# A matmul-heavy two-block kernel on one core: the second product of both MLPs by Strassen's seven block products

## The reference

```python
u = rmsnorm(h, mlp_norm_g[layer])
h = h + jnp.square(jax.nn.relu(u @ w_ff1[layer])) @ w_ff2[layer]   # 1024 -> 4096 -> 1024
```

## Time and profile before

| | |
|---|---|
| median of 3 runs | 3369.88 us (3363.81 to 3376.24) |
| profiled execution | 3384.9 us, span 3383.1 us |
| mean granted clock of TensorE | 0.886 of 2.4 GHz |
| expert gathering | about 158 to 1650 us |
| mixer of block two | about 1905 to 2298 us |
| first MLP on PE | 2371.9 to 2751 us |
| second MLP on PE | 3014.2 to 3374 us |

### The profile page before, as it was taken

The page is one execution under the profiler, slowest core; times in us unless marked ns, Lnnn a source line. Parts: engine busy times, 40 slices in busy tenths (PEclk is TensorE's granted clock), DMA queues, the critical chain, the costliest instruction groups (busy, mean ns, idle before and its releaser), DMA issues.

```text
span 3383.1 us, 44457 instructions
## 1 busy us (share of the span) xinstructions
PE 2793.3 (83%) x17412; PEld 2350.0 (69%) x17412; DVE 1711.5 (51%) x3924; ACT 1665.9 (49%) x3325; POOL 1140.7 (34%) x886
## 2 busy tenths in 40 slices
PE   6577877777678767577779888889999999999999
PEld 4465666565656556455468777778999997778887
DVE  6496969596877778445344455563200123621010
ACT  2167676778677767589644222223323222533231
POOL 0023333333333333233133222223645542156463
PEclk8687788788977888588889899999999999999999
DMA  5299999999999999999413000002233321023332
GB/s 187 72 399 354 370 399 401 382 372 403 405 368 361 415 403 413 416 405 397 181 50 75 14 1 1 1 1 63 77 92 88 94 69 57 1 75 99 89 99 75
DMA packets 287523, 695.75 MB, mean 206 GB/s; under 512 B 27664, under 2 KB 207299, under 8 KB 221651
## 3 DMA queue, kind: packets, MB, share of 16 engines
q0 software_dynamic: 73728, 536.90, 39.4%
q1 hardware_dynamic: 213587, 156.02, 14.5%
HBM read 689.72 MB, written 3.15 MB: 205 GB/s over the span
## 4 chain that ended last, share of the span: by engine, by line
PE 54%; DVE 21%; DMA 11%; ACT 10%; issue 3%; POOL 0%; SPq 0%; DVEq 0%; ACTq 0%; POOLq 0%
PE PS L1808 29%; DMA ring<-in_peer_uv,eidx 10%; DVE ring L1508 6%; PE PS L916 5%; ACT ring L1123 3%; PE PS L972 2%; DVE acc L2645 1%; PE PS L1707 1%; PE PS L1710 1%; PE PS L793 1%; PE PS L1700 1%; PE PS L766 1%; DMA W<-in_peer_wq 1%; PE PS L1829 1%; ACT L1116 1%
## 5 line engine op out<-in xcount | busy, mean ns | idle before, releaser
L916 PE MATMUL PS<-C,ring 128*128 128x128 f32 x4096 | 703.2, 324 | 336.4 <-ACT ring L1123 335.3
L916 PEld LDWEIGHTS PS<-C,ring 128*128 128x128 f32 x4096 | 560.9, 166 | 499.1 <-ACT ring L1123 449.8
L721 POOL DMA_INDIRECT ring<-in_peer_uv,eidx x512 | 487.3, 952 | 1154.0 <-PE PS L916 973.1
L1508 DVE CUSTOM_DVE_ANT_0 ring<-ring,PS 128x1024 f32<-128x1024 f32 x512 | 619.5, 1215 | 314.7 <-DMA ring<-in_peer_uv,eidx 309.5
L1123 ACT ACTIVATE ring<-ring,act_d 128x512 f32<-128x512 f32 x1024 | 683.4, 714 | 16.7
L1808 PE MATMUL PS<-held_uH,GW 128*128 128x264 f32 (+1 forms) x3008 | 662.4, 315 | 17.7 <-POOL BIG_value L2363 11.0
L2349 POOL TENSOR_TENSOR GW<-held_wr,GW 128x1024 fp32r<-128x1024 f32 x178 | 429.6, 2415 | 422.5 <-ACT GW L2114 422.5
L1808 PEld LDWEIGHTS PS<-held_uH,GW 128*128 128x128 f32 x3008 | 504.3, 194 | 58.0 <-issue 20.0
L1808 PE MATMUL PS<-BIG_value,GW 128*128 128x264 f32 (+1 forms) x1504 | 448.3, 313 | 0.0
L1808 PE MATMUL PS<-hid,GW 128*128 128x264 f32 (+1 forms) x2304 | 366.5, 321 | 0.0
L1808 PEld LDWEIGHTS PS<-hid,GW 128*128 128x128 f32 x2304 | 332.3, 188 | 33.7
(11 more groups left out here) (484 smaller groups left out, 3722.0 us busy)
## 6 DMA issues: line engine op xcount, KB each, us to landing
held_wr<-in_w_ff SPq DMA_DIRECT2D x128, 512.0 KB, 4.1
wqr<-in_peer_wq SPq DMA_DIRECT2D x32, 512.0 KB, 8.3
W<-in_peer_wq SPq DMA_DIRECT2D x31, 512.0 KB, 8.7
held_wr<-in_w_in_ab SPq DMA_DIRECT2D x18, 512.0 KB, 3.8
ring<-in_peer_uv,eidx POOLq DMA_INDIRECT x512, 9.7
BIG<-in_w_in SPq DMA_DIRECT2D x4, 1536.0 KB, 11.4
held_wr<-in_w_qkv_c SPq DMA_DIRECT2D x12, 512.0 KB, 3.7
w_out<-in_w_out SPq DMA_DIRECT2D x1, 4096.0 KB, 18.3
```

The costliest lines, as they stand in the source:

```text
L721: e.indirect_dma_start(out=ring[:, i % RING, :], out_offset=None, in_=pairs, in_offset=bass.IndirectOffsetOnAxis(ap=eidx[:, blk % 2, k:k + ...
L916: ins = e.matmul(bank[6 + j // 4][:, j % 4 * P:(j % 4 + 1) * P], row[:, j * P:(j + 1) * P], ident, start=(k == 0 and j % 4 == 0), stop=(k ...
L1508: e.tensor_tensor_reduce(row, row, hn, 1.0, 0.0, ALU.mult, ALU.add, act[:, k:k + 1]).then_inc(*n.up(e_dot))
```

## The change

1. **Second product.** The hidden width is worked in four quarters in place of two halves (8 units of the first product, then the second product of that quarter). For a pair of output tiles, p = 0 to 3, the 2x2 blocks (two output tiles; two halves of 512 contraction rows; two halves of the columns, 264 or 256) are multiplied with seven products in Winograd's form of Strassen's scheme in place of eight. Each of the seven (`A11, S1, A12, S2, S3, S4, A22`) is 4 blocks x 3 matmuls of half the columns, into one PSUM bank. DVE forms the weight sums S1 to S4 (`weight_sum`, 128x512 each) and two of the seven low parts (`weight_low`, S2 and S4); POOL keeps five low parts, ACT all seven high parts, all of 128x512. The sums lie where the low part goes, so S1's low part waits until S2's sum is formed. On the hidden side DVE forms T1 to T4 from half tiles (`hidden_sums`) and their low parts (`hidden_lows`), ACT the high parts. `combined` adds the products to the residual: 12 DVE operations on half tiles; ACT copies the first product to SBUF (`keep`).
2. **Weights.** Slots are taken by halves, six ahead (`Item.needs`), and a raw tile is freed by its last low part and by S4's sum.
3. **Mixer.** DVE's decay differences come one turn sooner; L1691's transposes and ACT's copy L2068 come one turn later.
4. **Fillers.** 30 matmuls of 512 columns that nobody reads (`warm`): in the front of block 0 twice 5 behind `drive`, 2 before the gate, 3 before L839 and 3 before the turns; 7 at the end of the tail; 5 at the start of block two.

```diff
+    def warm(e, few, bk, lhs, rhs):
+        for _ in range(few):
+            e.matmul(bk, lhs, rhs, start=True, stop=True)
...
+        def strassen(sp, p, ready):
...
+            for j, y in enumerate((0, 1, 2, 4, 5, 3, 6)):
...
+                if freed[bk]:
+                    e.wait_ge(*freed[bk])
+                freed[bk] = read[it.part]
+                e.wait_ge(*w_lov.at(lows_to[i]) if it.by_vector else (w_lo, lows_to[i]))
+                hi, lo = (r(z) for z in places(it)[0:2])
+                for k in range(4):
+                    if ready:
+                        e.wait_ge(*ready[y][k])
+                    for w_, x_ in ((0, 0), (0, 1), (1, 0)):
+                        ins = e.matmul(bank[bk][:, 0:w], (hi, lo)[w_][:, k * P:(k + 1) * P], r((XH, XL)[x_][:, y, k, 0:w]),
+                                       start=(k == 0 and w_ == 0 and x_ == 0), stop=(k == 3 and w_ == 1))
+                ins.then_inc(*up(g_done))
...
@@ second_pool, low
+            if it.part == "S1":
+                e.wait_ge(*w_sum.at(4 * it.group + 2))
...
@@ second_vector
+        def hidden_sums(sp, m):
...
+            t2, t3, t4 = (Xv[:, y, k, 0:w] for y in (4, 5, 6))
+            e.tensor_tensor(t3, half(m, 1), half(k, 1), ALU.subtract).then_inc(*up(dve))
+            e.wait_ge(*now(dve))
+            e.tensor_tensor(t2, t3, half(k, 0), ALU.add).then_inc(*up(dve))
+            e.wait_ge(*now(dve))
+            e.tensor_tensor(t4, half(m, 0), t2, ALU.subtract).then_inc(*up(th_sum))
...
+        def combined(sp, p, g, squares):
...
+            if p:
+                weight_low(g, "S4")
+            e.wait_ge(g_done, at + 2)
+            e.tensor_tensor(h22, h22, p5, ALU.add)
+            e.tensor_tensor(h12, h12, p5, ALU.add).then_inc(*up(f_out))
+            e.wait_ge(*f_kept.at(g + 1))
+            e.tensor_tensor(h11, h11, k1, ALU.add).then_inc(*up(dve))
+            e.wait_ge(g_done, at + 3)
+            e.wait_ge(*now(dve))
+            e.tensor_tensor(h11, h11, p2, ALU.add).then_inc(*up(f_out))
+            if more:
+                weight_sum(more, "S1")
+            e.wait_ge(g_done, at + 4)
+            e.tensor_tensor(v1, k1, p6, ALU.add).then_inc(*up(f_out))
+            e.wait_ge(*now(f_out))
+            e.tensor_tensor(h22, h22, v1, ALU.add)
+            e.tensor_tensor(h21, h21, v1, ALU.add)
+            e.tensor_tensor(h12, h12, v1, ALU.add).then_inc(*up(dve))
+            e.wait_ge(*now(dve))
+            e.wait_ge(g_done, at + 5)
+            e.tensor_tensor(h22, h22, p7, ALU.add)
+            e.tensor_tensor(h21, h21, p7, ALU.add).then_inc(*up(f_out))
+            if more:
+                weight_sum(more, "S2")
...
+            e.tensor_tensor(h12, h12, p3, ALU.add).then_inc(*up(h_res))
+            if more:
+                weight_sum(more, "S3")
...
+            e.tensor_tensor(h21, h21, p4, ALU.add).then_inc(*up(h_res))
+            if more:
+                weight_sum(more, "S4")
+                weight_low(more, "S2")
...
@@ delta_tensor
             ins.then_inc(*up(x_pe[d]))
+            yield
             e.wait_ge(x_dve[d], dv + 4)
             Am = v4(w_["b1"])
             for h in range(4):
                 ins = e.transpose(B[0:c, h * c:(h + 1) * c], Am[:, h], ident2[0:c, 0:c])
             ins.then_inc(*up(x_pe[d]))
-            yield
...
```

More of the change, by code:

```diff
@@ L130 @@
 NAT = 6
+PRODUCTS = ("A11", "S1", "A12", "S2", "S3", "S4", "A22")
+LOW_S = ("S2", "S4")
 Z_AT, ZOUT, XST_IN, XST, DRIVE0 = 5, 17, 18, 19, 20
@@ L1788, in gemm @@
                 e.wait_ge(*freed[b])
+            if sp.parts == 2 and freed[b + 1]:
+                e.wait_ge(*freed[b + 1])
             freed[b] = nxt(reader)
@@ L2109, in high, with split, output @@
         def high(i):
[L2111 to L2122, removed]
+            it = items[i]
+            if it.part and it.part[0] == "S":
+                e.wait_ge(*w_sum.at(4 * it.group + int(it.part[1])))
+            else:
+                e.wait_ge(d_f[it.raw % NW], loaded[it.raw])
+            if it.needs:
+                e.wait_ge(g_done, it.needs)
+            e.copy(r(places(it)[0]), source(it)).then_inc(*up(w_hi))
+        def split(done):
+            while count["split"] < limit[0] and items[count["split"]].needs <= done:
+                high(count["split"])
+                count["split"] += 1
+        def output():
+            count["unit"] += 1
+            split(count["unit"] - 1)
         def out_bank(sp=ALL):
@@ L2347, in low, with split, output @@
         def low(i):
+            it = items[i]
+            if it.by_vector:
+                return
             e.wait_ge(w_hi, i + 1)
[L2349 to L2356, removed]
+            if it.part == "S1":
+                e.wait_ge(*w_sum.at(4 * it.group + 2))
+            if it.part == "S3":
+                e.wait_ge(*w_sum.at(4 * it.group + 3))
+            hi, lo, _ = places(it)
+            e.tensor_tensor(r(lo), source(it), hi, ALU.subtract).then_inc(*up(w_lo))
+        def split(done):
+            while count["split"] < limit[0] and items[count["split"]].needs <= done:
+                low(count["split"])
+                count["split"] += 1
+        def output():
+            count["unit"] += 1
+            split(count["unit"] - 1)
         def low_half(dst, value_, hi, mine=True):
@@ L2539, in second_vector, with output @@
         count = {"unit": 0, "out": 0, "hi": 0, "sum": 0}
-        def output(units=1, sp=ALL):
-            count["unit"] += units
+        def output(sp=ALL):
+            count["unit"] += 1
             count["out"] += 1
@@ L2590, in norm, with residual @@
                 low_half(sp.cut(uL[:, k, :]), sp.cut(uT[:, k, :]), sp.cut(uH[:, k, :]), k in LOW_V)
-        def residual(units, squares, sp=ALL):
+        def residual(sp=ALL):
             for m in range(8):
-                b = output(units, sp)
-                if squares and m >= 2:
+                b = output(sp)
+                if m >= 2:
                     add_square(m - 1, sp)
```

282 lines of the change are left out of this document (234 added, 48 removed).

## The result

The changed kernel takes 3434.37 us in the median of 4 runs (3430.93 to 3435.94), the kernel before on the same chip 3369.39 (3363.81 to 3376.24): ratio 1.0185, 95% interval 1.0163 to 1.0208. It is slower by 65 us, and the forecast was 3430. A second set of runs of the same kernel gave 1.0182 (1.0160 to 1.0203). The profiled execution took 3430.93 us, with a span of 3429.1.

The account below looks back on a forecast made before the run. PE bounds the MLPs before; after, DVE and POOL excluding one another set the second products' pace. MLPs +77, mixer -12, fillers -5 make +60 on 3370, so 3430 us, range 3330 to 3475.

Parts of the forecast that it names:

- PE's saving of 41 us: Both MLPs' second products: seven products in place of eight take 23 us off PE in layer one, 18 in the last.
- The exclusion of DVE and POOL: Second products: DVE operations with two SBUF inputs and POOL lows take turns; 512 columns hold 1.15 us (POOL), 0.55 (DVE).
- Steady pair 12.5 (12.4) us: Second product's later pairs of output tiles take 12.5 us, in the last layer 12.4, against PE's own 10.25 (9.9).
- the walk: Tracing one pair through four queues: DVE never idle, 8.5 us its own work, 4.0 behind POOL.
- First pair 16.5 (16.9), second 13.4 (13.3): Turn from first to second product: first two pairs take 16.5 and 13.4 us; last layer 16.9 and 13.3.
- MLPs +34 and +43 = +77: Second products, four quarters a layer: layer one 34 us longer with the last squares, last layer 43, together 77.
- Mixer -12 and fillers -5: Earlier decay differences win 2.5 us in each of five mixer chunks, 12 us; fillers in PE's gaps win 5.
- (a): Rival, second products: the exclusion doesn't bind and PE sets the pace, pairs of 10.25 us; 3315 to 3330 us; 20%.
- (c): Rival, second products: PE's clock also falls after each first pair's gap, 22 us more; 3452, to 3475 us; 22%.
- (b): Rival, in between: pairs of 11 to 11.7 us, MLPs lose 0 to 30 us; 3355 to 3385 us; 13%.
- (d): Rival, mixer: the mixer change does nothing; 3442 us, counted within the main case, no chance of its own.
- the main case: The forecast itself, second products slowed by the exclusion: 3430 us, with its own scatter 3390 to 3445; 45%.

Follow-up runs that it names:

- the two kernels with fills: Changed kernel with POOL writing zeros in place of the product weights' low parts, one fill each (3344.66 us) or three fills each (3358.06 us); single runs.
- three fills: Changed kernel with three zero fills by POOL in place of each of its product weights' low parts: 3358.06 us, single run.

## Why the prediction was right

- **PE's saving of 41 us:** the sizes held. Where products follow one another, twelve matmuls of 264 columns take 1.46 us (0.122 each) and twelve of 256 take 1.42 (0.118, as priced). None of it arrived in the changed kernel.
- **The exclusion of DVE and POOL, 0.55 and 1.15 us:** held to 0.01 us, shown by the alternation and by the two kernels with fills. It costs the MLPs 823.5 - 748.8 = 75 us with POOL held as long, 78 with one fill.
- **Steady pair 12.5 (12.4) us:** 12.0, so the walk was 0.5 too long. DVE is full as said, but it is held up some 3.6 us a pair and not 4.0 (its operations' durations less those they have alone), which leaves 8.4 for its own work and not 8.5. In the walk S2's and S4's low parts ended 3.4 us after the first was asked; they take 2.21 here, since POOL stood idle for 0.50 us, waiting for ACT. In return S1's sum, free in the walk, was caught and took 1.25 us. The `keep` add was caught, as walked (0.84). DVE and POOL, the steady pair before the one above:

```profile
2423.79 2.21 DVE L2812 TENSOR_TENSOR GW<-GW_value,GW 128x512 fp32r<-128x512 f32 x2
...
2426.60 0.84 DVE L2853 TENSOR_TENSOR BIG<-BIG 128x264 f32<-128x264 f32 x1
...
2427.89 1.25 DVE L2803 TENSOR_TENSOR GW_value<-held_wr 128x512 f32<-128x512 f32 x1
```

```profile
2425.35 3.25 POOL L2525 TENSOR_TENSOR GW<-held_wr,GW 128x512 fp32r<-128x512 f32 x2 [0.50 <-ACT GW L2249]
```

- **First pair 16.5 (16.9), second 13.4 (13.3):** 16.5 to 16.7 (16.9 to 17.3), and 13.5 to 14.0 (12.9 to 13.3). The gaps of 2.7, 2.1, 0.7 and 0.8 us were 2.6, 1.7, 0.9 and 1.0, from start to start of the products less 1.46 each (the idle times in brackets are shorter, as PE also waits inside a product). Of the first pair's 6.3 us over 10.2, product lows against sums are 2.7 (13.8 with three fills), hidden lows another 2.0 (11.8), and 1.6 is what is left for the order of the queues.
- **MLPs +34 and +43 = +77:** +37.4 and +38.3 = +75.7. In layer one a quarter lost 7.2 to 7.4 us instead of 8.1, the last one, with the squares, 11.4 where I had 10. What I had not seen stands behind it: PE waits 4.76 us for the last squares before the next norm's sums, where before it waited 0.60 for ACT's.

```profile
2755.00 3.68 PE L1945 MATMUL PS<-held_C,BIG 128*88 128x1 f32 x24 [4.76 <-DVE BIG L2757]
```

In the last layer the pairs came out 0.85 us a quarter under the walk.
- **Mixer -12 and fillers -5:** alone -16 and -8, inside the bounds; together 24 us in a kernel with the old MLPs, 6 in one with the new. My 17 lies between. The fillers' 5 us was my estimate, and no run shows that term: the runs show the 8 us alone, the 4.8 us of the gate's and the output product's matmuls, and 0.86 us for a filler at the full clock, in the gaps. Why there is less beside the new MLPs, if it is not noise, is open.
- **Sum:** +60 forecast, +65 measured: the MLPs' 76 less some 11, where I had 77 less 17.
- **The rivals.** (a), the exclusion doesn't bind, is out: sums stand at 1.38 us, and its 3315 to 3330 us isn't reached even with POOL's reads for the second product gone (3339). (c), the clock falls, is right in its mechanism and wrong in its price. The traces give no frequency, only the share of the full clock: over the 5.9 us from 2371.90 on, which begin with the matmuls of the earlier trace rows at 0.22 us, it is 0.50. The clock fell to 0.89 over the first two pairs in five of eight quarters, but PE waits for DVE there anyway: in the last layer these two pairs take 30.20 to 30.23 us with the fall and 30.22 without, in layer one 30.6 and 30.0 to 30.1. That is 1 us in all, not 22. With one fill in place of each of POOL's product low parts, PE sets more of the pace and a fall does cost: 25.0 to 25.2 us for the two pairs in the four quarters with it, 24.3 to 24.4 in the four without. Where the gap is 8 us, it is 15 in all. (b) is out with its pairs of 11 to 11.7. (d) is out in the kernel with the old MLPs, by the mixer edit's 16 us alone; in the changed kernel, where both small edits together bring 6, it isn't told from the main case.

What the traces add to the forecast is how little could be won. With fills in place of POOL's low parts for the second product the MLPs stand at 378.0 + 351.5 = 729.5 us against 746.2 with eight products: 17 of PE's 41 us. The turns from first to second product keep most of the rest: each of the eight quarters has a first and second pair 2.4 to 2.8 us over PE's pace, 20 us. Behind the last pair of layer one the wait for the squares keeps some 5 more. And the best version with all the arithmetic of the seven products in place, four low parts on DVE and the adds from PSUM, loses 0.9%. The kernel to keep is the one with the old MLPs, the mixer edit and the fillers.

## What to carry to other kernels

Fewer matmuls pay only if what makes their operands fits beside them: count the time that the engines' operations exclude one another as if it were one more engine (here 1.15 us for POOL's and 0.55 for DVE's of 128x512), before the busy time of each alone. Where both DVE and POOL prepare operands, put an input into PSUM where it can be (8 us less in the MLPs here), or keep the operations that read two SBUF operands on one engine (four low parts on DVE and the adds from PSUM: steady pairs of 10.20 us in place of 12.0), and then look at the turn between stages: an operation moved to the other queue also stands behind all that is queued there. The 8 us gap on PE cost some 2 us more than its length, as the clock fell to 0.50 in it; the fillers in it kept the clock up and still lost time, as they ran 5.3 us over its end. Measure small edits in the kernel that will keep them: here they brought 24 us in one and 6 in the other.

## What the runs showed of the hardware

A low part of POOL held back by DVE costs POOL as well: 1.74 us in place of 1.28, and the two take turns, one of each in 1.70 us. A POOL fill of 128x512 takes 0.53 us and leaves a DVE sum that starts 0.04 us later at 0.69 us (one fill each; DVE in the second line):

```profile
2406.88 0.53 POOL L2526 MEMSET GW<- 128x512 f32 x1 [0.54 <-ACT GW L2249]
2406.92 0.69 DVE L2806 TENSOR_TENSOR GW_value<-held_wr,GW_value 128x512 f32<-128x512 f32 x1
```

A filler of float32 with 512 columns shows as two matmuls of 0.43 us at the full clock, where one of fp32r takes 0.231. And a fall of the clock to 0.89 over two pairs cost nothing that could be seen in the last layer of the changed kernel, where DVE's and POOL's queues set the pace (30.20 to 30.23 us with it, 30.22 without).
